# Column groups of 512, 512 and 48 in place of 358, 358 and 356 in the projections of a hybrid decoder layer

## What is computed

```python
h = rmsnorm(x, norm_w)
z, xbc, dt_raw, qkv, a_raw, b_raw, gate, mg_ssm, mg_gdn = split_cols(h @ w_in, IN_SIZES)
xbc, new_ssm_conv = causal_dwconv(xbc, s_ssm_conv, ssm_conv_w)
qkv, new_gdn_conv = causal_dwconv(qkv, s_gdn_conv, gdn_conv_w)
...
# SSD scan and gated-delta scan over the tokens, output projections, residual
...
h = rmsnorm(x, norm_w)
gt, up = split_cols(h @ w_up, (D_FF, D_FF))
gt, new_conv = causal_dwconv(gt, s_conv, conv_w)
return x + (jax.nn.silu(gt + conv_b) * up) @ w_down, new_conv
```

## Time and profile before

| what | value |
|---|---|
| median of 3 runs | 3392.09 us |
| the profiled execution, its own time | 3393.49 us |
| its span, from the first to the last instruction | 3391.7 us |
| PE (TensorE matmul) busy | 3031.9 us, 89% of the span, 19120 matmuls |
| PEld (TensorE weight loads) busy | 2852.0 us, 84% |
| DVE (VectorE) busy | 1556.2 us, 46% |
| ACT (ScalarE) busy | 969.1 us, 29% |
| mean granted TensorE clock | 0.936 of full |

### The profile page before, as it was taken

The page is one execution under the profiler, slowest core; times in us unless marked ns, Lnnn a source line. Parts: engine busy times, 40 slices in busy tenths (PEclk is TensorE's granted clock), DMA queues, the critical chain, the costliest instruction groups (busy, mean ns, idle before and its releaser), DMA issues. The chain is left out here.

```text
span 3391.7 us, 53016 instructions
## 1 busy us (share of the span) xinstructions
PE 3031.9 (89%) x19120; PEld 2852.0 (84%) x19120; DVE 1556.2 (46%) x2378; ACT 969.1 (29%) x1944; POOL 417.8 (12%) x578
## 2 busy tenths in 40 slices
PE   3799999999999788888888587999888999997998
PEld 2799999999999777776777227999888999997998
DVE  5455555511111277777777443455353332323443
ACT  2223222221211244443444100333232111112332
POOL 2000000000000122233222232000010000000100
PEclk7899999999999899998999666999998999998999
DMA  2222222222242323223430523664431122124443
GB/s 77 81 89 89 99 91 89 89 101 89 89 139 96 87 53 71 62 62 73 92 81 16 181 96 109 236 208 157 163 108 66 62 70 99 57 75 172 169 143 111
DMA packets 230884, 347.36 MB, mean 102 GB/s; under 512 B 146648, under 2 KB 165416, under 8 KB 230496
## 3 DMA queue, kind: packets, MB, share of 16 engines
q1 hardware_dynamic: 225392, 324.24, 30.1%
q0 software_dynamic: 5360, 21.40, 1.8%
HBM read 252.39 MB, written 93.22 MB: 102 GB/s over the span
## 5 line engine op out<-in xcount | busy, mean ns | idle before, releaser
L534 PE MATMUL pps<-h_hi,pwh 128*128 128x358 f32 (+1 forms) x2112 | 688.4, 326 | 15.3 <-DVE pwl L599 15.3
L534 PE MATMUL pps<-h_lo,pwh 128*128 128x358 f32 (+1 forms) x2112 | 690.1, 327 | 0.0
L534 PE MATMUL pps<-h_hi,pwl 128*128 128x358 f32 (+1 forms) x2112 | 687.4, 325 | 0.0
L534 PEld LDWEIGHTS pps<-h_hi,pwh 128*128 128x128 f32 x2112 | 397.4, 188 | 15.7 <-issue 15.7
L534 PEld LDWEIGHTS pps<-h_hi,pwl 128*128 128x128 f32 x2112 | 398.8, 189 | 0.0
L534 PEld LDWEIGHTS pps<-h_lo,pwh 128*128 128x128 f32 x2112 | 397.6, 188 | 0.0
L1681 PE MATMUL u_ps<-f_hi,up_wh 128*128 128x358 f32 (+1 forms) x1056 | 345.3, 327 | 8.0 <-DVE up_wl L1673 8.0
L1681 PE MATMUL u_ps<-f_lo,up_wh 128*128 128x358 f32 (+1 forms) x1056 | 344.9, 327 | 0.0
L1681 PE MATMUL u_ps<-f_hi,up_wl 128*128 128x358 f32 (+1 forms) x1056 | 344.2, 326 | 0.0
L599 DVE TENSOR_TENSOR pwl<-pw,pwh 128x1024 fp32r<-128x1024 f32 x88 | 107.7, 1225 | 508.1 <-ACT pwh L547 501.5
L1681 PE MATMUL merge_ps<-merge_yh,merge_wh 128*128 128x358 f32 (+1 forms) x576 | 190.3, 330 | 30.8 <-DVE merge_yl L1827 23.8
(11 more groups left out here) (435 smaller groups left out, 5308.9 us busy)
## 6 DMA issues: line engine op xcount, KB each, us to landing
projected<-pO SPq DMA_DIRECT2D x88, 536.0 KB, 2.9
pw<-in_w_in SPq DMA_DIRECT2D x88, 512.0 KB, 3.7
merge_w<-in_w_out SPq DMA_DIRECT2D x72, 512.0 KB, 3.5
down_w<-in_w_down SPq DMA_DIRECT2D x48, 704.0 KB, 4.2
up_w<-in_w_up SPq DMA_DIRECT2D x44, 512.0 KB, 4.0
chunk<-projected SPq DMA_DIRECT2D x5, 3744.0 KB, 16.8
scan_chunk<-projected SPq DMA_DIRECT2D x5, 3744.0 KB
wo_w<-in_w_o SPq DMA_DIRECT2D x24, 512.0 KB, 3.5
```

What stands on the lines that cost most here:

```text
L534: ins = pe.matmul(ps[:, 3 * u + n, 0:cn], l[u][:, k, :], r[:, k, c0:c0 + cn], start=(k == 0 and a == 0), stop=(k == KD - 1 and a == 2))
```

## The change

A second table of groups, `PCOL`, takes the place of `NCOL` in the three phases, in the products and in all that read their banks. The number of matmuls, weight loads, copies and activations stays what it was; only their widths change. In the up projection the wait for the last activations moves from ahead of the third group to ahead of the second, since the second now reaches from column 512 to column 1023. The diff, cut to its core:

```diff
 NCOL = ((0, 358), (358, 358), (716, 356))
+PCOL = ((0, 512), (512, 512), (1024, 48))
...
@@ gates_phase, TensorE
-            for n, (c0, cn) in enumerate(NCOL):
+            for n, (c0, cn) in enumerate(PCOL):
...
-                pe.wait_ge(ev["gathered"].sem, ev["gathered"].at(0, min(3, -(-(t * C + n) // NCOL[0][1]))))
+                pe.wait_ge(ev["gathered"].sem, ev["gathered"].at(0, sum(c0 < t * C + n for c0, _ in PCOL)))
...
@@ project_phase, ScalarE
-                    for n, (c0, cn) in enumerate(NCOL):
+                    for n, (c0, cn) in enumerate(PCOL):
                         cp = min(cn, TP - c0)
                         act.activation(U[:, u, 3 + c0:3 + c0 + cp], ps[:, 3 * u + n, 0:cp], ACT.Copy).then_inc(evacuated[u].sem, 1)
                     act.activation(
-                        seqs(U[:, u, :])[:, :, 3:7], ps[:, 3 * u + 2, TP - 716:TP - 716 + TS].rearrange(
+                        seqs(U[:, u, :])[:, :, 3:7], ps[:, 3 * u + 2, TP - PCOL[2][0]:TP - PCOL[2][0] + TS].rearrange(
...
@@ up_phase, TensorE
-                    for n, (c0, cn) in enumerate(NCOL):
-                        if n == 2:
+                    for n, (c0, cn) in enumerate(PCOL):
+                        if n == 1:
                             pe.wait_ge(n_lo.sem, n_lo.at(0))
...
```

More of the change, by code:

```diff
@@ L2316, in body @@
                 act.wait_ge(new_got.sem, new_got.ahead(j))
-                for n, (c0, cn) in enumerate(NCOL):
+                for n, (c0, cn) in enumerate(PCOL):
                     cp = min(cn, TP - c0)
                     act.activation(U[:, 2 + c0:2 + c0 + cp], ps[:, n, 0:cp], ACT.Copy).then_inc(evacuated.sem, 1)
-                act.activation(seqs(U)[:, :, 2:6], ps[:, 2, TP - 716:TP - 716 + TS].rearrange(
+                act.activation(seqs(U)[:, :, 2:6], ps[:, 2, TP - PCOL[2][0]:TP - PCOL[2][0] + TS].rearrange(
                     "p (b t) -> p b t", t=NT), ACT.Copy).then_inc(evacuated.sem, 1)
```

## The result

The changed kernel takes 3670.53 us, the median of four runs (3665.8 to 3671.17), against 3390.77 us before, now also of four runs: **8.2% slower**, ratio 1.0819, 95% interval 1.0805 to 1.0833. That is 280 us where 260 were forecast, inside the range.

A forecast was written before the change was run, and what follows sets the result against it. TensorE's matmuls, one behind the other, were taken to bound the input and up projections. 250 us for the matmuls and 10 us for the clock, on 3393.5 us, gave 3654 us; range 3578 to 3721.

The forecast's parts named there:

- The bound and the count: Input and up projection: TensorE busy throughout, so each phase lasts as long as its matmuls in a row; 3168 triples.
- triples: One matmul of each of a tile's three column groups; 2112 in input projection, 1056 in up projection, 490.4 ns before.
- Narrow matmuls cost their load: Both projections: a matmul of 48 columns can't hide its load of 128 weight columns and costs 111.4 ns, down from 162.9.
- Wide matmuls: Both projections: a matmul of 512 columns costs 229 ns, within 220.0 to 234.2, where 358 columns cost 163.75.
- the fixed reading: Wide matmuls in both projections: the 14.6 ns beyond the stream are per matmul, so 512 columns cost 227.9 ns.
- The clock: Both projections: narrow runs make the clock fall to half a few times, 6 falls of about 1.7 us, 10 us.
- Rival B: Both projections: the clock falls in each of the 132 tiles, 224 us in place of 10, 3868 us; chance 0.08.
- Sum: Both projections: 2 x 229 + 111.4 - 490.4 = 79.0 ns per triple, x 3168 = 250 us; 184 to 283 us.
- The earlier wait in the up projection: First tile of the up projection: the wait for the last activations finds its work done, 0 us.
- The gates: Gates, 24 triples with weights of 48 columns: 10 ns more each, 0.2 us in all, taken as 0.
- C: Both projections: narrow loads hide after all, made further ahead or spared for repeated weights; 3400 or 3343 us; chance 0.03.
- D: Both projections: wide matmuls cost by the instruction, not the column; -163 us, 3230 us; chance 0.02.

The follow-up runs named there:

- The interleaved kernel: Against the changed kernel: in the input projection the groups become the innermost loop, so each narrow matmul stands between wide ones; 3661.77 us, ratio 1.0790 to the kernel before.

## Why the prediction was right

- *The bound and the count.* Both phases were as long as their matmuls one behind the other, and 3168 triples times the change of one give the result. Shown: nothing else grew, no wait came, and the up projection alone has a third.
- *Narrow matmuls cost their load.* Taken as 111.4 ns from the scan's fp32 rows, measured 111.5 with fp32r. Shown by weights of 64 columns (57 ns), by those of 48 in the gates (45.5), and by 176 streamed columns at the same 110. That the figure came out so exactly is in part luck, since the row it was taken from can't tell a load from a stream. Its 14 matmuls also streamed 128 fp32 columns, and in the scan before that stream takes as long even with lighter weights, of 104 columns:

```profile
1210.68 1.04 PE L879 MATMUL scan_ps<-c_ident,scan_chunk 128*104 128x128 f32 x8
1211.56 0.33 PE L1086 MATMUL scan_ps<-scan_X,scan_TL 104*96 104x96 f32 x2
```

Eight take 0.88 us, 110 ns each, where the load of 104 columns alone cost 88.1. Only the row with a single streamed column showed a load by itself, and it gave 108.5. Its own pace was a little slower, since the first of its 16 starts came early as at the seam above: the others stand 91.7 ns apart, which is 113 for 128 columns.

- *Wide matmuls: mis-sized.* The step "I take 229, near the fixed reading, because the extra time doesn't grow with the width in those rows" took bf16 and half-rate streams for evidence on an fp32r stream. It measured 231.5: of the extra time most goes with the columns. 2 x 2.5 ns x 3168 = 16 us of the 20 us that were missing. By the formula of the Trainium skill, page "TensorE: Matmul & The Clock Gate", section "Back-to-back issue gap", the estimate at this width is 215.8 ns; the trace disagrees, with 231.5, so of the two the row was the better guide.
- *The clock.* Nine falls where six were taken. Each cost 1.55 us, so the nine are 14 us, where 10 were counted. The six were a guess between 0 and 132 that no row supported; that it came so near is luck. Rival B, a fall in each tile, fails by the factor of 15, but its mechanism is real: twice the run makes it fall every time.
- *Sum.* 574.6 - 490.4 = 84.2 ns x 3168 = 267 us, 14 for the clock and 1 for the gates: 282, against 280 measured.
- *Costs put at nothing.* The earlier wait in the up projection doesn't show in PE's waits, and ScalarE and VectorE worked the same time in the phases. The gates took 1.0 us more and not 0.2 (first matmul to first transpose 56.29 to 71.32, before 56.28 to 70.32); the clock, at half when they begin, also rose some 1 us later there (first start at full clock 62.30, before 61.28).
- *Rivals C and D* fall on the rows: a narrow matmul needs 111.5 ns and not under 50, a wide one 231.5 and not under 189.5. The interleaved kernel closes C's last way out, that a load might be made earlier.

None of the kernels is shown to beat the one before; 404, 404 and 264 is the same as it within the interval.

## What to carry to other kernels

Where every matmul brings its own weight load, the narrowest group must stream at least as long as a load. Above that width (264 columns and more here) the split of the columns hardly matters; below it (176 and 48) every matmul of the group is charged the full load. Cut evenly rather than filling banks and leaving a rest: the same number of instructions and columns cost 280 us more here. Ask of a narrow group in a dense phase also what the clock will make of it.

## What the runs showed of the hardware that was not expected

- An fp32r stream at full clock cost about 6 ns and 0.44 ns a column (123.8 ns at 268 columns, 183.3 at 404, 202.9 at 448, 231.5 at 512), though 2.4 GHz would be 0.417. It isn't the weight load: with loads of 48 columns it was 231.4 ns at 512. What the extra time is stays open; no kernel here tries it.
- PE's busy share alone doesn't tell what the clock makes of a stretch: with PE recorded as busy for all of 5.10 us, in matmuls of 48 columns, the clock fell to half and stayed there for 6.7 us. With 176 columns, in rows of 2.65 us, it never fell in the input projection.
- A load was made one ahead and no further: between two wide matmuls the narrow one still cost a load, whose record begins only 0.02 to 0.03 us ahead of its matmul's.
- A load of 128 columns cost 111.5 ns at full clock and some 210 at half.
